# A transformer stack on one core: one pattern of zero products for every FFN and mixer panel, and two heads' products that alternate

## What is computed

```python
def swiglu(h, w_gate_up, w_down):
    gate, up = jnp.split(h @ w_gate_up, 2, axis=-1)
    return (jax.nn.silu(gate) * up) @ w_down
# FFN: 1024 -> 2 x 2816 -> 1024, eight of them
# Fourier mixer: fft2(...).real @ w_out;   S5 mixer: val, gate = split(g @ w_glu); val * sigmoid(gate)

# selective mixer, state space part (16 heads of 64, one chunk of 256 tokens)
decay = segsum_exp(adt)
cb = jnp.einsum('bclgn,bcsgn->bcgls', cc, bc)
y_diag = jnp.einsum('bcgls,bcgels,bcsgep->bclgep', cb, decay, x)
```

## Time and profile before

| | before |
|---|---|
| median of 3 runs | 2603.05 us (2591.95 to 2603.62) |
| the profiled execution | 2603.65 us |
| its span, first to last instruction | 2601.8 us |
| mean granted TensorE clock | 0.982 |
| TensorE matmuls busy | 2495.0 us (96%) |
| VectorE busy | 1778.3 us (68%) |
| ScalarE busy | 1259.3 us (48%) |
| DMA | 164 GB/s from memory over the span |

### The profile page before, as it was taken

The page is one execution under the profiler, slowest core; times in us unless marked ns, Lnnn a source line. Parts: engine busy times, 40 slices in busy tenths (PEclk is TensorE's granted clock), DMA queues, the critical chain, the costliest instruction groups (busy, mean ns, idle before and its releaser), DMA issues.

```text
span 2601.8 us, 54597 instructions
## 1 busy us (share of the span) xinstructions
PE 2495.0 (96%) x23182; PEld 2436.6 (94%) x23182; DVE 1778.3 (68%) x2300; ACT 1259.3 (48%) x1508; POOL 216.0 (8%) x246
## 2 busy tenths in 40 slices
PE   7999759999999899999999999999999999999998
PEld 7999759999999889989999999999999998999998
DVE  5988966556555666657666669876657667986665
ACT  5434445334566653344344346565335335665433
POOL 5000050003000100000000000500000000320000
PEclk9999879999999999999999999999999999999999
DMA  5553014555677735535545544434555554443553
GB/s 214 183 189 125 19 67 176 180 191 169 187 174 182 174 117 193 192 133 189 192 172 206 193 171 154 147 130 165 191 183 185 191 193 147 152 147 146 179 194 127
DMA packets 65839, 430.76 MB, mean 166 GB/s; under 512 B 8288, under 2 KB 11360, under 8 KB 15904
## 3 DMA queue, kind: packets, MB, share of 16 engines
q1 hardware_dynamic: 58864, 410.30, 44.1%
q0 software_dynamic: 6000, 17.46, 4.5%
q10 hardware_dynamic: 832, 0.92, 0.1%
HBM read 426.45 MB, written 1.15 MB: 164 GB/s over the span
## 4 chain that ended last, share of the span: by engine, by line
PE 88%; DVE 7%; ACT 3%; issue 1%; DMA 0%; DVEq 0%; ACTq 0%
PE psum L2020 26%; PE psum L2022 26%; PE psum L2021 26%; DVE w_lo L1332 1%; ACT w_hi L847 1%; PE psum L2070 1%; PE psum L2235 1%; PE psum L2141 1%; PE psum L2384 1%; DVE h L1351 1%; PE psum L2372 1%; DVE h_lo L1340 1%; PE psum L2362 1%; PE psum L2124 0%; PE psum L2328 0%
## 5 line engine op out<-in xcount | busy, mean ns | idle before, releaser
L2020 PE MATMUL psum<-h_hi,w_hi 128*128 128x256 f32 x4320 | 1215.1, 281 | 16.4 <-DVE h_lo L1376 9.6
L2021 PE MATMUL psum<-h_lo,w_hi 128*128 128x256 f32 x4320 | 1205.0, 279 | 0.0
L2022 PE MATMUL psum<-h_hi,w_lo 128*128 128x256 f32 x4320 | 1204.6, 279 | 0.0
L847 ACT ACTIVATE w_hi<-raw 128x2048 fp32r<-128x2048 f32 x387 | 741.2, 1916 | 857.1 <-PE psum L2022 857.1
L1332 DVE TENSOR_TENSOR w_lo<-raw,w_hi 128x2048 fp32r<-128x2048 f32 x387 | 886.8, 2292 | 386.9 <-ACT w_hi L847 386.5
L2020 PEld LDWEIGHTS psum<-h_hi,w_hi 128*128 128x128 f32 x4320 | 816.1, 189 | 26.0 <-issue 20.8
L2021 PEld LDWEIGHTS psum<-h_lo,w_hi 128*128 128x128 f32 x4320 | 815.8, 189 | 0.6 <-issue 0.5
L2022 PEld LDWEIGHTS psum<-h_hi,w_lo 128*128 128x128 f32 x4320 | 815.5, 189 | 0.0
L2020 PE MATMUL psum<-act_hi,w_hi 128*128 128x256 f32 x1536 | 427.3, 278 | 0.7 <-DVE act_lo L1895 0.7
L2021 PE MATMUL psum<-act_lo,w_hi 128*128 128x256 f32 x1536 | 426.1, 277 | 0.0
L2022 PE MATMUL psum<-act_hi,w_lo 128*128 128x256 f32 x1536 | 426.0, 277 | 0.0
(11 more groups left out here) (342 smaller groups left out, 2386.5 us busy)
## 6 DMA issues: line engine op xcount, KB each, us to landing
raw<-in_panels SPq DMA_DIRECT2D x387, 1024.0 KB, 4.8
arena<-bias_by_distance POOLq DMA_DIRECT2D x32, 384.0 KB, 6.2
x<-in_x SPq DMA_DIRECT2D x1, 1024.0 KB, 5.6
arena<-in_s_cbd POOLq DMA_DIRECT2D x4, 256.0 KB, 3.0
arena<-in_s_b SPq DMA_DIRECT2D x1, 1024.0 KB, 15.2
arena<-in_s_c SPq DMA_DIRECT2D x1, 1024.0 KB, 17.2
hidden<-in_s_cbd POOLq DMA_DIRECT2D x4, 256.0 KB, 2.8
arena<-arena POOLq DMA_DIRECT2D x32, 32.0 KB, 1.9
```

The costliest lines, as they stand in the source:

```text
L847: a.activation(w_hi[:, s, :], raw[:, s, :], ACT.Copy).then_inc(hi_ready, 1)
L2020: t.matmul(o, w[0], xin[0], start=start, stop=False, skip_group_check=True)
L2021: t.matmul(o, w[0], xin[1], start=False, stop=False, skip_group_check=True)
L2022: return t.matmul(o, w[1], xin[0], start=False, stop=stop, skip_group_check=True)
```

## The change

Two parts of the order of TensorE's instructions change; VectorE, ScalarE, GpSimd and SyncE keep theirs.

The table by FFN goes, and one table `PACE` takes its place: wide at (0, 0), wide at (0, 4), narrow with 2 columns at (1, 4), all in panel 1 of the stage. All eight FFNs, the two Fourier mixers and the GLU use it. The last FFN had these already.

In `ssd_pair` the products of the two heads take turns, and TensorE waits for both heads' operands before the first of them.

```diff
-        FFN_LEADS = [{(1, 0): 1}, {(1, 0): 2}, {(0, 4): 0}, {(0, 2): 0, (1, 2): 0}, {(0, 0): 3, (1, 0): 0},
-                     {(0, 0): 2}, {(0, 0): 3, (1, 0): 1}, {(0, 0): 3, (0, 4): 3, (1, 4): 0}]
+        PACE = {(0, 0): True, (0, 4): True, (1, 4): False}
...
-            def lead(o, start=True, form=0):
-
-
-                z = zeros[:, :].bitcast(F32)
-                if form == 0:
+            def lead(o, start, wide):
+
+
+                if wide:
+                    t.matmul(o[:, 0:E], zeros[:, :], zeros[:, 0:E], start=start, stop=True, skip_group_check=True)
+                else:
+                    z = zeros[:, :].bitcast(F32)
                     t.matmul(o[:, 0:2], z, z[:, 0:2], start=start, stop=True, skip_group_check=True)
...
-                project(n0 + 1, 1, led=FFN_LEADS[f])
+                project(n0 + 1, 1, led=PACE)
...
-                    project(st["n0"] + p, p, parts=None if p else (dft_lo_ready, f * KT // 2), frees=(p == 3), led={(0, 0): 0} if p == 1 else None)
+                    project(st["n0"] + p, p, parts=None if p else (dft_lo_ready, f * KT // 2), frees=(p == 3), led=PACE if p == 1 else None)
...
-                    project(st["n0"] + p, p, parts=None if p else (s5_g_lo_ready, 0), frees=(p == 7), led={(0, 0): 0} if p == 1 else None)
+                    project(st["n0"] + p, p, parts=None if p else (s5_g_lo_ready, 0), frees=(p == 7), led=PACE if p == 1 else None)
...
                 def ssd_pair(j):
+
                     if j:
                         t.wait_ge(y_raw, 8 * i + j)
-                    for e in range(2):
-                        hd = 2 * j + e
-                        t.wait_ge(decay_used, SSD_H * i + hd + 1)
-                        o = bank[6][e * SSD_P:(e + 1) * SSD_P, :]
-                        heads = slice(hd * SSD_P, (hd + 1) * SSD_P)
-                        t.matmul(o[:, 0:P], mx.xt[:, 0, heads], mx.m[:, e, 0, 0:P], start=True, stop=True)
-                        t.matmul(o[:, P:S], mx.xt[:, 0, heads], mx.m[:, e, 0, P:], start=True, stop=False)
-                        last = t.matmul(o[:, P:S], mx.xt[:, 1, heads], mx.m[:, e, 1, P:], start=False, stop=True)
+                    t.wait_ge(decay_used, SSD_H * i + 2 * j + 2)
+                    for tt_, to, first, stop in ((0, slice(0, P), True, True), (0, slice(P, S), True, False), (1, slice(P, S), False, True)):
+                        for e in range(2):
+                            hd = 2 * j + e
+                            last = t.matmul(bank[6][e * SSD_P:(e + 1) * SSD_P, to], mx.xt[:, tt_, hd * SSD_P:(hd + 1) * SSD_P],
+                                            mx.m[:, e, tt_, to], start=first, stop=stop)
                     last.then_inc(yp_ready, 1)
```

More of the change, by code:

```diff
@@ L2022, in mm3 @@
                 return t.matmul(o, w[1], xin[0], start=False, stop=stop, skip_group_check=True)
-            def lead(o, start=True, form=0):
-                z = zeros[:, :].bitcast(F32)
-                if form == 0:
-                    t.matmul(o[:, 0:2], z, z[:, 0:2], start=start, stop=True, skip_group_check=True)
[L2030 to L2036, removed]
+            def lead(o, start, wide):
[3 more added lines that the diff above has]
+                    z = zeros[:, :].bitcast(F32)
+                    t.matmul(o[:, 0:2], z, z[:, 0:2], start=start, stop=True, skip_group_check=True)
             def weights(n, lo, width=P):
```

## The result

The changed kernel takes 2577.04 us (median of 5 runs, 2570.61 to 2579.16); the kernel before, beside it on the same chips, 2599.36 us (5 runs, 2591.95 to 2603.62). The ratio is 0.9897, with a 95% interval of 0.987 to 0.9925, so 22.3 us less by the medians (19.5 to 33.8 by the interval). The profiled executions are 2576.94 and 2603.65 us, 26.7 us apart. The prediction had 21.2 us less and 2582 us; 2577.04 is at the low end of its range.

What follows compares the result with a forecast made beforehand. TensorE was taken to bound the kernel, with a product under way for 96% of the span. Pace -20.25, zero products +1.4, heads -3.9 and clock +1.5 sum to -21.2 us from 2603.65, so 2582 us, range 2577 to 2597.

Steps and rivals of the forecast that it cites:

- the base: Starting time for the forecast: the profiled execution's 2603.65 us, taken as within 0.6 us of the median.
- The pace: FFN 1, 2 and 6: 1500 products each gain 4.5 ns, 6.75 us per FFN, -20.25 us in all.
- VectorE would just fit in FFN 1: FFN 1, where VectorE also prepares the S5 mixer: 19.2 us of time for 19.09 us of work, costed at nothing.
- The reason given for the wide products: Behind the sum-of-squares wait: a wide product at (0, 0) brings the stream to one alignment where the narrow one works.
- The rival in which the second wide spoils it: At (1, 4) the narrow product fails: four slow FFNs give 2609.4 us, seven 2629.6; chance 0.08.
- The zero products: FFNs and three mixers: the new pattern's zero products and later switch cost +1.4 us in sum, +0.39 per mixer.
- The heads in turn: Seven later pairs in each of two mixers: alternating heads saves 0.28 us a pair, -3.9 us.
- a rival of its own: Panels behind each pair happen to run at the fast pace: 2.8 us more gain, 2579.6 us; chance 0.12.
- The rule of the Trainium skill that stood against it: Pairs of heads: alternating on the same rows gains nothing, the 3.9 us are missing, 2586.3 us; chance 0.04.
- The clock in the second mixer's first pair: Second mixer's first pair: a longer idle piece lowers the clock, 13 products missing, +1.5 us, or nothing.

Runs made afterwards that it cites:

- e7: Changed kernel without the wide product at (0, 4): 2587.19 us, ratio 0.9939.
- e3: Changed kernel without both wide products, the narrow one kept at (1, 4): 2611.00 us, ratio 1.0037.
- e4: Changed kernel without the narrow product, both wide ones kept: 2631.63 us, ratio 1.0107.
- e1: Changed kernel with the heads of a pair one after the other as before, so the zero products alone: 2581.77 us, ratio 0.9919.
- e12: The kernel of e1 again, on the same chip as e11: 2579.76 us, ratio 0.9921.
- e9: Changed kernel with VectorE making the last pair's sum y ahead of the next panel's w_lo: 2577.39 us against 2597.67 for the kernel before.
- e11: The changed kernel itself, unedited, on the same chip as e12: 2577.33 us, ratio 0.9915.
- e2: Kernel before with only the heads in turn, its zero products kept: 2601.80 us, ratio 0.9983.
- e5: Changed kernel with each selective mixer's first pair in the order of before, with separate waits: 2577.65 us in one run.
- e6: Changed kernel with GpSimd's second round held until VectorE has made the first pair's factors: 2574.37 us, ratio 0.9881.
- e8: Changed kernel with one wide product at (0, 0) and the narrow one at (0, 1) instead of the three: 2634.74 us, ratio 1.0119.

## Why the prediction was off by a few microseconds, step by step

The mechanism was right, and the time came out 5.0 us below the 2582 that was forecast. Two steps failed.

The first is the base: "Against the profiled execution's own 2603.65 us this is 2582.4, and that execution is within 0.6 us of the median, so 2582". The median was one of three runs that lay 11.7 us apart; with five it is 2599.36, and the 46 later runs of this kernel lie between 2580.47 and 2618.63. From 2599.36 the same 21.2 us give 2578.2, 1.1 above what was measured. So 3.7 of the 5.0 us are the base's and not the change's.

The second is in the sum. Between the two profiled executions 26.7 us fell where 21.2 were forecast. The clock outside the places that the change reorders was put at nothing without a look, and measured -4.2 in the S5 mixer; and the clock's +1.5 in the second mixer came out as -1.7. The heads' -3.9 was too large, which hid part of this: that their errors partly cancel is luck. Term by term:

**The pace** (-20.25) measured -19.7 with its zero products, against -20.8 with them: a product gained 4.3 ns between FFN 1's panels 5 and 36 (175.66 to 169.23 us) rather than 4.5. This was read rightly from the counts. That VectorE would just fit in FFN 1 held too: the tightest panel, at 93.02, had its `w_lo` 0.50 us ahead.

**The reason given for the wide products** was half right. "A wide product at (0, 0), right behind the wait, brings the stream to one alignment" fell with e7. What holds is that narrow alone is a matter of luck (e3), wide alone does nothing (e4), and with two wides and a narrow at (1, 4) all FFNs are fast in all eight profiles, of six kernels, that have them: 64 of 64. The rival in which the second wide spoils it had it backwards. That all are fast is seen in profiles alone: one of e1's runs without a profile took 2588.95 us, where the same kernel in e12, on another chip, never took more than 2580.55, so an FFN may still fall slow now and then; no profile shows it.

**The zero products** (+1.4) were sized rightly: +0.39 in each of the three mixers (0.39 forecast), and +0.33, +0.03 and +0.17 in FFN 3, 4 and 5 (0.34, 0.04, 0.17).

**The heads in turn** (-3.9) gained per pair what was forecast, 0.27 for 0.28. What failed is "14 later pairs of 0.28", -3.9: behind the first pair's panel the two state space parts are 1.7 us shorter. The seventh panel of each mixer gave back 0.39 and 1.24 us at the last pair, since TensorE now came to the sum y before VectorE had got to it (0.39 and 0.77 us of waiting; e9 shows it) and, in the second mixer, to the last pair's factors as well (0.39). On the other side, one later panel of the first mixer and two of the second ran at the fast pace, 7.11 us instead of 7.33, which I had as a rival of its own. The net in the medians is 2.4 us, by e11 and e12. The rule of the Trainium skill that stood against it ("TensorE: Matmul & The Clock Gate", Part 3, "What overlaps and what doesn't": weight loads overlap with products in flight only when the row group differs) would give 1.08 us for the pair; the trace has 0.81 for the 12 passes, all on the same rows, so it does not agree.

**The clock in the second mixer's first pair** (+1.5) is the term that failed in sign for the profiled execution: -1.7 was measured in that panel. The clock did fall in e2, at 2259.4, as forecast, and in all six profiles with the joint wait in which VectorE was late (see e5): so, as far as these profiles go, the reason stands and its size too, about 1.1 to 1.6 us over before's 17.0. Its condition didn't hold. I had taken VectorE's end at this place as given, and in the changed kernel GpSimd's products came when three of the four factors were done. Before, VectorE, GpSimd and TensorE:

```profile
2257.22 1.55 DVE L1864 SCALAR_TENSOR_TENSOR arena<-arena 128x256 f32<-128x256 f32 x1
2254.66 2.49 POOL L782 TENSOR_TENSOR arena<-arena,rope 32x512 f32<-32x512 f32 x2 [3.46 <-DMA arena<-arena]
2259.09 0.43 PE L2481 MATMUL psum<-arena,hidden 128*64 128x128 f32 x2 [0.86 <-DVE arena L1865]
```

and in the changed kernel:

```profile
2231.81 0.48 DVE L1864 SCALAR_TENSOR_TENSOR arena<-arena 128x256 f32<-128x256 f32 x1
2232.21 1.18 DVE L1865 SCALAR_TENSOR_TENSOR arena<-arena 128x128 f32<-128x128 f32 x1
2232.08 2.45 POOL L782 TENSOR_TENSOR arena<-arena,rope 32x512 f32<-32x512 f32 x2 [4.82 <-DMA arena<-arena]
```

e6 shows that this meeting of VectorE and GpSimd sets how long TensorE is idle. It isn't a sure gain: the panel took 7.65 to 7.68 us in four profiles with the changed pace (the changed kernel, e11, e1, e5), but 9.75 in e12, whose kernel is e1's.

**What was left out** are the 4.2 us of the S5 mixer. I had looked at the clock only where the change reorders something. Before's profiled execution carried a stretch of 6.8 us at 1.2 GHz that the changed one didn't, worth about 3.1 of them. The 4.2 us are the largest part of the difference between forecast and profile. Whether the new pace ahead of this place removed the stretch or the execution happened not to have it stays open: of five profiles with a slow FFN 1 three have it in full (before, e2, e3) and two don't (e4, e8), and of nine with a fast one only e5 has half of it. That before scatters over 11.7 us and the changed kernel over 8.6 fits with this and with FFNs that take either pace from run to run, but no run shows which of the two it was in an execution without a profile.

## What to carry to other kernels

When a stream of equal instructions has two speeds in one trace, count its records in equal stretches before looking for a wait; and when a small instruction seems to cure it, ask in how many entries of the stream it was seen, since a cure that depends on what stands ahead of it can also undo a good state. Before taking one profiled execution as the kernel's time, see how far its runs scatter. A saving on the bounding engine is worth what the engine behind it can follow: look at the first and the last of a row of equal places, where the queue of that other engine holds something else. Compare the granted clock of all stretches between two profiles before giving a difference to the change.

## What the hardware showed that I had not expected

- **A narrow product switches the pace both ways.** In four places (e2 in FFN 1 and 4, e3 in FFN 4 and 7) the stream behind the wait was at 113.3 ns already, and the narrow product took it to 117.8, four of four. That is why slow after it doesn't mean that it did nothing.
- **The failing cases differ in the weight loads, by a nanosecond or two.** In streams at 117.8 ns, and leaving out e8's, the narrow product failed six times in all profiles together and worked some 120 times. Take the last two weight loads of the stream ahead of it and its own two. In five of the six failures they start 118, 117, 119 and 115 ns behind the load before, in the sixth 117, 118, 118 and 115; none of the working ones has either sequence. But the commonest working ones (118, 118, 117, 116 and 119, 117, 118, 115) differ from these by 1 or 2 ns, and the pattern was found afterwards, so it describes these cases. What in TensorE it reflects stays open.
- **VectorE stretched by GpSimd.** L1864 and L1865 take 0.48 and 0.34 us alone and up to 1.55 and 1.36 beside a GpSimd product of some 1.25 us. The Trainium skill ("SBUF — State Buffer", "SBUF: two separate sides") says that a VectorE operation with two SBUF inputs and a GpSimd operation that reads SBUF take turns, the loser blocked for the whole instruction. The trace agrees: 1.55 less 0.48 is 1.07 us, most of one product.
- **A few microseconds come and go.** The same kernel's panel with the first pair took 9.31 us in one profiled execution and 10.39 in another (the changed kernel and e11; with the panel behind it 18.16 and 18.56), and the S5 mixer's panel between 133.0 and 137.0 over eight profiles whose code is the same there. A difference of 2 us between two single profiles is no evidence for an edit.
